# Moving the gate projection behind attention and the SSM tables into attention, in a hybrid attention and S5 encoder layer

## The chip, the core and the metric

The kernel runs on one core of a Trainium2 chip. The metric is the time of one execution in microseconds (us), lower is better. The engines have these names in the rows: PE is TensorE (PEld its weight loads), DVE is VectorE, ACT is ScalarE, POOL is GpSimd, SP is SyncE, which here only issues DMAs. A name with a q behind it (SPq, PEq) is the sequencer of that engine.

## The reference, cut to what matters

One encoder layer over 2048 tokens of width 1024, all in float32. The parts that the change touches are these:

```python
h = rmsnorm(x, norm_mix_pre)
z = h @ w_in                            # 1024 x 3328: [q | k | v | u | gates]
q, k, v, u, gates = jnp.split(z, splits, axis=-1)   # 512, 128, 128, 512, 2048 columns
y_attn = windowed_gqa_sink(q, k, v, attn_sink) @ w_branch_attn     # |t - s| <= 128, 8 heads, 2 kv heads
y_ssm = s5_bidirectional(u, ...) @ w_branch_ssm     # scan in both directions, + D*u, GELU, GLU
g = jax.nn.sigmoid(gates.reshape(bsz, seq, 2, 1024))
merged = g[:, :, 0] * y_attn + g[:, :, 1] * y_ssm
# then w_out, a norm, and a gated feed-forward part of width 2816 with a 3-tap convolution
```

The S5 part has 32 groups of 16 channels with 64 complex states each. The kernel computes it in chunks of 8 tokens: tables of powers of the transition take a chunk's inputs into its state (`into`), a scan runs over the 256 chunk states, further tables take the state before a chunk to its outputs (`outof`), and `local` covers what tokens of one chunk do to each other.

## The kernel before, in words

Every large matrix product is made from split operands: `split_products` (L322) multiplies w_hi by x_hi, w_lo by x_hi and w_hi by x_lo, so three matmuls of 128x512 for each 128 rows of the contraction. A block of 128 output rows by 2048 tokens has 4 chunks of 512 tokens and 8 contraction steps, so 96 matmuls. `WeightStream` (L282) loads a block's weights (SyncE), rounds them to w_hi (L315) and subtracts to w_lo (L317) on VectorE, in two slots.

The stages run one after the other with a barrier between them (L64):

- `stage_project_in`: norm and transposition of x into `feat_hi` and `feat_lo`, which stay in SBUF for the stage, and then 26 blocks: 6 for q, k, v, 4 for u, 16 for the gates. Beside them GpSimd computes the bases of the SSM tables (`bases.compute`) from small parameters that SyncE loads, and VectorE takes one reciprocal in it (`bases.invert`). In the SyncE queue these small loads stand ahead of the weights of block 2, and in the VectorE queue the reciprocal stands ahead of splitting them.
- `ssm_tables` (tiles `st_`): VectorE and GpSimd compute `b_table` and `outof` with complex products (L1170 to L1175), TensorE transposes, ScalarE copies, TensorE makes the `kernels`, and 16 DMAs spread them into `local`.
- `chunks_into_states` (tiles `si_`): 128 matmuls take u into the states, copied by ScalarE and VectorE.
- `attention_and_scan` (tiles `at_`): 16 blocks of 128 queries and 8 heads. For a head TensorE computes scores (L1770), VectorE masks them (L1861), ScalarE takes exponentials (L1967), TensorE transposes them (L1780), ScalarE copies (L1976), and TensorE multiplies by v (L1794). GpSimd runs the backward scan by itself. VectorE runs the forward scan in pieces between the masks. A scan has 45 steps of four parts (`ChunkScan.part`, L2067 to L2072): 15 large steps inside blocks of 16 chunks, 15 small ones over the blocks, 15 large ones into the next block.
- `states_to_outputs` (tiles `so_`): 16 pairs of groups, matmuls with `local` and `outof`, GELU on ScalarE, 64 stores by SyncE.
- then `stage_branches` (tiles `br_`), `stage_out`, `stage_gate_up` and `stage_down`, which stay as they are.

The order on each engine is that of the code; nothing is scheduled by a program.

Of the kernel before, what the change touches and what calls it, by code (L numbers as in the profile page):

```python
# [21 lines left out]
F32 = mybir.dt.float32  # L22
F32R = mybir.dt.float32r
# [22 lines left out]
WARM_UP = 72  # L46
# [283 lines left out]
def stage_project_in(nc, x, gain, w_in, qkv, u_scratch, gate_scratch, bases):  # L330
# [3 lines left out]
    with ExitStack() as ctx:  # L334
# [10 lines left out]
        n_qkv, n_u, n_gate = qkv.shape[0] // P, SSM // P, 2 * D // P  # L345

        parts = [(0, n_qkv, qkv, "plain"), (n_qkv, n_u, u_scratch, "by chunk"),
                 (n_qkv + n_u, n_gate, gate_scratch, "sigmoid")]
        n_blocks = n_qkv + n_u + n_gate
# [9 lines left out]
        @block.sync  # L359
        def _(sync):  # L360
            nt.load(sync, ws, [(s, w_in, slice(s * P, (s + 1) * P)) for s in range(2)])

            sync.wait_ge(nt.turned, TILES + 2)
            bases.load(nc, sync)
            with sync.Fori(1, n_blocks // 2) as i:
                for s in range(2):
                    ws.load(sync, w_in, s, i * 2 + s, bass.ds((i * 2 + s) * P, P))

        @block.vector
        def _(dve):  # L370
            nt.vector(dve, turn_psum, ws)
            bases.invert(dve)
            with dve.Fori(1, n_blocks // 2) as i:
                for s in range(2):
                    ws.vector(dve, s, i, i * 2 + s)
# [23 lines left out]
        def _(act):  # L399
# [4 lines left out]
            for first, count, dest, kind in parts:  # L404
                dest_rows = dest.rearrange("(b p) t -> b p t", p=P)
                with act.Fori(0, count // 2) as i:
                    for s in range(2):
# [4 lines left out]
                        for c in range(CHUNKS):  # L412
# [9 lines left out]
                            func = ACT.Sigmoid if kind == "sigmoid" else ACT.Copy  # L422
                            act.activation(out, src, func).then_inc(chunk_free, 1)  # L423
# [964 lines left out]
def stage_mixers(nc, qkv, sink, attn_scratch, u_scratch, bases, ssm_d, y_scratch):  # L1388
# [3 lines left out]
    with ExitStack() as ctx:  # L1392
        m = Pool(nc, ctx, "sm")

        outof = [[m.sb(f"outof{d}{r}", [P, QS, POWERS, SSM_CH]) for r in range(2)] for d in range(2)]

        region = m.sb("region", [P, 2 * 2 * QS * P])
        u_region = m.sb("u_region", [P, GROUPS * SSM_J])
        u = u_region[:].rearrange("p (g j) -> p g j", g=GROUPS)
        into = region[:].rearrange("p (d q e r n) -> p d q e r n", d=2, q=QS, e=2, r=2)  # L1400
        local = m.sb("local", [P, GROUPS, LC])
        with ExitStack() as part:
            ssm_tables(nc, Pool(nc, part, "st"), bases, ssm_d, u_scratch, u, outof, into, local)

        states = [m.sb(f"states{d}", [P, 2, QS, SSM_J + 1]) for d in range(2)]
        scans = [ChunkScan(m, d, states[d], bases.leaps[d], d == 1) for d in range(2)]
        with ExitStack() as part:
            chunks_into_states(nc, Pool(nc, part, "si"), u, into, states)
        with ExitStack() as part:
            lost = attention_and_scan(nc, Pool(nc, part, "at"), region, u_region, qkv, sink, attn_scratch, scans)  # L1410
        with ExitStack() as part:
            states_to_outputs(nc, Pool(nc, part, "so"), region, u, lost, u_scratch, y_scratch, outof, local, states)


def ssm_tables(nc, m, bases, ssm_d, u_scratch, u, outof, into, local):
# [842 lines left out]
```

## Time and profile before

| | before |
|---|---|
| median of 3 runs | 3148.57 us (3147.24 to 3149.11) |
| the profiled execution, its own time | 3148.73 us |
| its span in the trace | 3147.2 us |
| mean granted TensorE clock, share of full speed | 0.957 |
| busy share of the span: PE, PEld | 90%, 73% |
| busy share: DVE, ACT, POOL | 37%, 23%, 16% |

The span reaches from the first to the last instruction; the profiled execution took 1.5 us more than that. A busy share is a mean over stages with different limits, and PE counts as busy while a matmul is in its pipeline, so the shares alone don't tell what a stage waits for. The stages have to be read one by one.

### The profile page before, as it was taken

To read this page: it belongs to the slowest core of one execution; us is meant where nothing else is said; L and a number is where in the kernel's file an instruction comes from. 1 tells how busy PE (TensorE), PEld (TensorE's weight loads), DVE (VectorE), ACT (ScalarE), POOL (GpSimd) and SP (SyncE) were. 2 spreads that over 40 slices of the span, in tenths; PEclk is the share of its full clock that TensorE was granted. 3 is DMA by queue.
4 is the path that set the end of the run, shared out by engine and by line. 5 is a ranking of instruction groups with operands and counts; after the bars stand their busy time and mean duration, and the time that the engine had idled before them with its cause. 6 is when DMAs were issued, how large, how long until landed. Compare 5 with 4: busy or idle time off the path is not lost. (4 is left out here: it accounts for less than half of the span.)

```text
span 3147.2 us, 36636 instructions
## 1 busy us (share of the span) xinstructions
PE 2831.1 (90%) x13014; PEld 2310.1 (73%) x13014; DVE 1161.7 (37%) x1392; ACT 709.8 (23%) x1144; POOL 509.1 (16%) x829
## 2 busy tenths in 40 slices
PE   6699999945898778989948999999999997999998
PEld 5588888835666557867847888888888885888886
DVE  5000000065999816434334322223223233224342
ACT  4012111122454324002123111111111112213221
POOL 2440000062788600001111000000000001000111
PEclk9899999977999989999969999999999998999999
DMA  4312212142111172435442111111111115434653
GB/s 127 81 60 80 78 62 80 52 89 27 48 59 47 34 186 104 170 136 181 145 122 81 53 33 53 53 47 53 34 52 53 47 40 165 116 96 126 178 165 122
DMA packets 298549, 278.18 MB, mean 88 GB/s; under 512 B 46592, under 2 KB 270080, under 8 KB 288768
## 3 DMA queue, kind: packets, MB, share of 16 engines
q1 hardware_dynamic: 253792, 160.94, 18.4%
q0 software_dynamic: 13248, 68.16, 6.1%
q10 hardware_dynamic: 31456, 48.42, 5.0%
q8 instruction: 28, 0.46, 0.1%
q14 instruction: 25, 0.20, 0.0%
HBM read 191.50 MB, written 83.89 MB: 88 GB/s over the span
## 5 line engine op out<-in xcount | busy, mean ns | idle before, releaser
L325 PE MATMUL gu_banks<-gu_feat_hi,gu_w_hi 128*128 128x512 f32 (+1 forms) x1408 | 549.4, 390 | 1.0 <-DVE gu_feat_lo L235 1.0
L327 PE MATMUL gu_banks<-gu_feat_lo,gu_w_hi 128*128 128x512 f32 (+1 forms) x1408 | 548.4, 389 | 0.0
L326 PE MATMUL gu_banks<-gu_feat_hi,gu_w_lo 128*128 128x512 f32 (+1 forms) x1408 | 548.3, 389 | 0.0
L325 PE MATMUL pi_banks<-pi_feat_hi,pi_w_hi 128*128 128x512 f32 (+1 forms) x832 | 326.8, 393 | 31.0 <-DVE pi_w_lo L317 30.0
L327 PE MATMUL pi_banks<-pi_feat_lo,pi_w_hi 128*128 128x512 f32 (+1 forms) x832 | 325.0, 391 | 0.0
L326 PE MATMUL pi_banks<-pi_feat_hi,pi_w_lo 128*128 128x512 f32 (+1 forms) x832 | 325.0, 391 | 0.0
L325 PEld LDWEIGHTS gu_banks<-gu_feat_hi,gu_w_hi 128*128 128x128 f32 x1408 | 264.6, 188 | 55.9 <-DVE gu_feat_lo L235 1.4
L327 PEld LDWEIGHTS gu_banks<-gu_feat_lo,gu_w_hi 128*128 128x128 f32 x1408 | 264.5, 188 | 55.2
L326 PEld LDWEIGHTS gu_banks<-gu_feat_hi,gu_w_lo 128*128 128x128 f32 x1408 | 264.6, 188 | 54.4
L325 PE MATMUL dn_y<-dn_w_hi,dn_f_hi 128*128 128x512 f32 x704 | 276.3, 393 | 23.4 <-DVE dn_w_lo L801 23.3
L326 PE MATMUL dn_y<-dn_w_hi,dn_f_lo 128*128 128x512 f32 x704 | 275.4, 391 | 0.0
L327 PE MATMUL dn_y<-dn_w_lo,dn_f_hi 128*128 128x512 f32 x704 | 275.3, 391 | 0.0
L315 DVE CAST gu_w_hi<-gu_w_raw 128x1024 fp32r<-128x1024 f32 x44 | 30.5, 693 | 619.2 <-PE gu_banks L327 619.2
L325 PEld LDWEIGHTS pi_banks<-pi_feat_hi,pi_w_hi 128*128 128x128 f32 x832 | 157.3, 189 | 64.0 <-issue 30.4
L504 ACT ACTIVATE gu_gate<-gu_banks 128x512 f32<-128x512 f32 x88 | 52.7, 601 | 596.2 <-PE gu_banks L327 596.2
L315 DVE CAST pi_w_hi<-pi_w_raw 128x1024 fp32r<-128x1024 f32 x26 | 18.1, 695 | 446.5 <-PE pi_banks L327 437.9
L423 ACT ACTIVATE pi_rows_out<-pi_banks 128x512 f32<-128x512 f32 x104 | 70.0, 676 | 496.3 <-PE pi_banks L327 496.3
L327 PEld LDWEIGHTS pi_banks<-pi_feat_lo,pi_w_hi 128*128 128x128 f32 x832 | 156.9, 189 | 32.9
L326 PEld LDWEIGHTS pi_banks<-pi_feat_hi,pi_w_lo 128*128 128x128 f32 x832 | 157.2, 189 | 32.4
L325 PEld LDWEIGHTS dn_y<-dn_w_hi,dn_f_hi 128*128 128x128 f32 x704 | 133.2, 189 | 53.2 <-issue 19.2
L557 POOL DMA_DIRECT2D f<-gu_conv x22 | 11.8, 535 | 936.5 <-DVE gu_conv L539 936.5
L327 PEld LDWEIGHTS dn_y<-dn_w_lo,dn_f_hi 128*128 128x128 f32 x704 | 133.1, 189 | 28.1
(237 smaller groups left out, 4237.7 us busy)
## 6 DMA issues: line engine op xcount, KB each, us to landing
dn_f_raw<-f SPq DMA_DIRECT2D x64, 704.0 KB, 5.9
f<-gu_conv POOLq DMA_DIRECT2D x22, 1024.0 KB, 4.1
gates<-pi_rows_out ACTq DMA_DIRECT2D x16, 1024.0 KB, 4.3
br_rows<-gates POOLq DMA_DIRECT2D x16, 1024.0 KB, 7.0
pi_w_raw<-in_w_in SPq DMA_DIRECT2D x26, 512.0 KB, 4.8
gu_w_raw<-in_w_ffn_gate SPq DMA_DIRECT2D x22, 512.0 KB, 3.8
gu_w_raw<-in_w_ffn_up SPq DMA_DIRECT2D x22, 512.0 KB, 3.8
dn_w_raw<-in_w_ffn_down POOLq DMA_DIRECT2D x22, 512.0 KB, 6.9
```

What stands on the lines that cost most here:

```text
L315: dve.tensor_copy(self.hi[:, s], self.raw[:, s]).then_inc(self.hi_ready, 1)
L325: pe.matmul(out, w_hi, x_hi, start=first, stop=False)
L326: pe.matmul(out, w_lo, x_hi, start=False, stop=False)
L327: return pe.matmul(out, w_hi, x_lo, start=False, stop=last)
L423: act.activation(out, src, func).then_inc(chunk_free, 1)
L504: act.activation(gate[:, 1 + c * BANK:1 + (c + 1) * BANK], banks[:, c, :], ACT.Copy)\
L557: pool.dma_start(f_rows[i], conv[:]).then_inc(stored, 16)
```

## The change

Three things are done together.

1. `stage_project_in` makes only the 10 blocks of q, k, v and u. The weights of blocks 2 and 3 are loaded and split ahead of the small loads and the reciprocal of the bases. Between later weight loads SyncE stores `feat_hi` and `feat_lo` to DRAM, 8 DMAs of 2 MB.
2. `attention_and_tables` replaces `ssm_tables` and the attention stage. The head loop is written out; a slot is one head of one block (128 slots). VectorE makes a piece of the table products in two of three slots (8 of the 16 columns, in groups of 4), GpSimd the other 8 columns in a row, TensorE puts the transpositions and kernel products into numbered slots, all through one PSUM bank `t_psum`. The warm-up of TensorE (72 transpositions) is gone. `outof` and `local` are stored to DRAM at the stage's end, all by SyncE.
3. `gates_and_states` (tiles `gs_`) makes the states, then the 16 gate blocks as 64 parts of 24 matmuls, token chunk by token chunk, so that the gate weights are loaded four times over (64 loads of 512 KB for 16). ScalarE rounds the weights and takes the sigmoid, VectorE subtracts. GpSimd and VectorE scan meanwhile, VectorE three parts for each gate part. Features come back from DRAM chunk by chunk; then `outof`, `local` and u, and the outputs follow without a barrier.

```diff
-        n_qkv, n_u, n_gate = qkv.shape[0] // P, SSM // P, 2 * D // P
+        n_qkv, n_u = qkv.shape[0] // P, SSM // P
...
+            for b in range(2, 4):
+                ws.load(sync, w_in, b % 2, b, slice(b * P, (b + 1) * P))
             sync.wait_ge(nt.turned, TILES + 2)
             bases.load(nc, sync)
-            with sync.Fori(1, n_blocks // 2) as i:
-                for s in range(2):
-                    ws.load(sync, w_in, s, i * 2 + s, bass.ds((i * 2 + s) * P, P))
+            for b in range(4, n_blocks):
+                ws.load(sync, w_in, b % 2, b, slice(b * P, (b + 1) * P))
+                if b % 2:
+                    continue
+                c = (b - 4) // 2
+                store_features(c)
...
+    DVE_COLUMNS = [slice(0, QS // 4), slice(QS // 4, QS // 2)]
+    POOL_COLUMNS = [slice(QS // 2, QS)]
+    C_AT = {10 + n: n for n in range(4)}
+    INTO_AT = {**{20 + 2 * n: n for n in range(8)}, **{38 + 2 * n: 8 + n for n in range(8)}}
+    KERNELS_AT = {**{56 + 2 * n: n for n in range(K_BANKS)}, **{78 + 2 * n: K_BANKS + n for n in range(K_BANKS)}}
...
+                if slot - 1 in KERNELS_AT:
+                    keep_kernels(KERNELS_AT[slot - 1])
+                elif slot == DIAG_AT:
+                    add_diagonal()
+                if slot % 3 != 2:
+                    next(own_tables, None)
...
+        for n in range(N_PARTS):
+            c, s = n // N_BLOCKS, n % 2
+            if n % N_BLOCKS == 0:
+                pe.wait_ge(feat_in[c % 2], (c // 2 + 1) * 2 * KD * 16)
+            pe.wait_ge(w_lo_ready, n + 1)
+            if n >= 2:
+                pe.wait_ge(gate_free, n - 1)
+            for k in range(KD):
+                done = split_products(pe, banks[:, 6 + s, :], w_hi[:, s, k], w_lo[:, s, k],
+                                      feat[c % 2][:, 0, k], feat[c % 2][:, 1, k], k == 0, k == KD - 1)
+            done.then_inc(gate_done, 1)
...
+        def split_hi(n):
+            act.wait_ge(w_raw_in[n % 2], n // 2 * 16 + 16)
+            if n >= 2:
+                act.wait_ge(gate_done, n - 1)
+            act.activation(w_hi[:, n % 2], w_raw[:, n % 2], ACT.Copy).then_inc(w_hi_ready, 1)
...
+        for n in range(N_PARTS):
+            if n + 2 < N_PARTS:
+                split_lo(n + 2)
+            for _ in range(3):
+                next(own_scan, None)
```

Three places of the instruction order show it. First SyncE in the input projection: ahead, the weights of block 2 and later (`pi_w_raw`) stand behind the loads of the bases' parameters (`pi_normed`).

```order
L1276 DMA pi_normed<-in_b_im_f 128x16x16
L1276 DMA pi_normed<-in_b_re_b 128x16x16
L1276 DMA pi_normed<-in_b_im_b 128x16x16
L365 UNCONDITIONAL_BRANCH
L365 ISA
L301 ISA
L301 DMA pi_w_raw<-in_w_in 128x8x128
```

In the changed kernel two weight loads stand ahead of them, and the feature stores follow between the later ones:

```order
L300 DMA pi_w_raw<-in_w_in 128x8x128 x2
L1280 DMA pi_normed<-in_lam_re_f 128x16x1
L1282 DMA pi_normed<-in_lam_im_f 128x16x1
L1286 DMA pi_normed<-in_log_dt_f 64x16x1 x2
L1280 DMA pi_normed<-in_lam_re_b 128x16x1
L1282 DMA pi_normed<-in_lam_im_b 128x16x1
L1286 DMA pi_normed<-in_log_dt_b 64x16x1 x2
L1290 DMA pi_normed<-in_b_re_f 128x16x16
L1290 DMA pi_normed<-in_b_im_f 128x16x16
L1290 DMA pi_normed<-in_b_re_b 128x16x16
L1290 DMA pi_normed<-in_b_im_b 128x16x16
L300 DMA pi_w_raw<-in_w_in 128x8x128
```

The loads for blocks 2 and 3 have moved from behind the parameters to ahead of them. Second VectorE in attention, before: a mask (two ISA rows, L1861) and then one part of the scan, for each head.

```order
L1861 ISA sm_region,at_neg_top<-at_s_psum,sm_region,at_neg_sinks 128x385
L1861 ISA at_neg_top 128x1
L2067 TENSOR_TENSOR sm_by_im<-sm_states,bases 128x512
L1861 ISA sm_region,at_neg_top<-at_s_psum,sm_region,at_neg_sinks 128x385
L1861 ISA at_neg_top 128x1
L2069 TENSOR_TENSOR sm_states<-sm_states,sm_by_re 128x32x16
```

In the changed kernel a piece of the tables stands where the scan part stood, and in each third slot nothing:

```order
L1867 ISA at_neg_scores,at_neg_top<-at_s_psum,at_bias,at_neg_sinks 128x385
L1867 ISA at_neg_top 128x1
L1434 TENSOR_TENSOR at_table_temp<-bases 128x4x128
L1867 ISA at_neg_scores,at_neg_top<-at_s_psum,at_bias,at_neg_sinks 128x385
L1867 ISA at_neg_top 128x1
L1867 ISA at_neg_scores,at_neg_top<-at_s_psum,at_bias,at_neg_sinks 128x385
L1867 ISA at_neg_top 128x1
L1437 TENSOR_TENSOR at_outof<-at_outof,at_table_temp 128x512
```

The third place is VectorE in the new stage: the scan parts (L2352 to L2357) stand three by three between the subtractions that make w_lo (L2272), each for one gate part.

```order
L2272 TENSOR_TENSOR gs_w_lo<-gs_w_raw,gs_w_hi 128x1024
L2352 TENSOR_TENSOR bases<-gs_states,bases 128x512 x2
L2354 TENSOR_TENSOR gs_states<-gs_states,bases 128x32x16
L2272 TENSOR_TENSOR gs_w_lo<-gs_w_raw,gs_w_hi 128x1024
L2356 TENSOR_TENSOR gs_states<-gs_states,bases 128x16x16
L2357 TENSOR_TENSOR gs_states<-gs_states,bases 128x16x16
```

The scan has moved from between the masks to between the weight splits of the gates.

## Rows read from the trace of the kernel before

**Rows 1.** Windows by stage: us, busy time (instructions), TensorE clock, DMA, GB/s.

```profile
0.00:123.95 123.95, 67.36 (x320) 54.17 (x321) 44.98 (x39) 38.94 (x57) 25.48 (x91) 0.88 0.41 111
123.95:267.90 143.95, 143.95 (x626) 118.95 (x627) 13.63 (x14) 19.53 (x26) 64.36 (x199) 0.98 0.23 73
267.90:648.60 380.70, 380.70 (x1680) 314.91 (x1678) 30.72 (x32) 55.62 (x78) 0.00 (x0) 1.00 0.20 66
648.60:654.30 5.70, 0.00 (x0) 0.00 (x0) 0.00 (x0) 0.60 (x1) 0.00 (x0) 0.68 0.45 184
654.30:758.80 104.50, 33.45 (x208) 30.57 (x208) 71.57 (x37) 15.05 (x32) 70.67 (x29) 0.66 0.49 71
758.80:791.80 33.00, 30.08 (x128) 25.81 (x128) 27.18 (x66) 24.26 (x64) 0.01 (x1) 0.93 0.00 1
791.80:804.20 12.40, 9.75 (x72) 9.52 (x73) 10.09 (x15) 1.28 (x1) 8.57 (x11) 0.86 0.33 96
804.20:1095.70 291.50, 253.20 (x1470) 182.06 (x1470) 275.56 (x553) 143.34 (x400) 231.63 (x220) 0.98 0.15 45
1095.70:1099.70 4.00, 0.00 (x0) 0.00 (x0) 0.00 (x0) 0.59 (x1) 0.00 (x0) 0.77 0.22 66
1099.70:1149.50 49.80, 49.09 (x320) 36.36 (x320) 0.00 (x0) 10.84 (x17) 0.00 (x0) 0.95 0.73 117
```

**Rows 2.** Timeline of TensorE where block 2 begins: start us, us, idle before.

```profile
123.95 0.79 PE L325 MATMUL pi_banks<-pi_feat_hi,pi_w_hi 128*128 128x512 f32 x1 [30.00 <-DVE pi_w_lo L317]
```

**Rows 3.** Timeline of VectorE, two weight splits one block apart.

```profile
148.16 0.69 DVE L315 CAST pi_w_hi<-pi_w_raw 128x1024 fp32r<-128x1024 f32 x1 [22.14 <-PE pi_banks L327]
...
169.92 0.69 DVE L315 CAST pi_w_hi<-pi_w_raw 128x1024 fp32r<-128x1024 f32 x1 [19.80 <-PE pi_banks L327]
```

**Rows 4.** Timeline of SyncE's DMA issues: last weights of the projection, `local`.

```profile
116.82 447.33 SPq L301 DMA_DIRECT2D pi_w_raw<-in_w_in  x24
...
738.34 9.54 SPq L1464 DMA_DIRECT2D sm_local<-st_kernels  x8
```

**Rows 5.** DMA issues: count, KB each, median us from issue to landing.

```profile
f<-gu_conv POOLq DMA_DIRECT2D x22, 1024.0 KB, 4.1
...
pi_w_raw<-in_w_in SPq DMA_DIRECT2D x26, 512.0 KB, 4.8
```

**Rows 6.** Timeline of the weight loads, scores of two heads, one after the other.

```profile
944.86 0.30 PEld L1770 LDWEIGHTS at_s_psum<-sm_region 128*128 128x128 f32 x2
...
946.51 0.30 PEld L1770 LDWEIGHTS at_s_psum<-sm_region 128*128 128x128 f32 x2
```

**Rows 7.** Timeline of VectorE, the reciprocal that each query block has once.

```profile
936.98 0.19 DVE L1894 RECIPROCAL at_share<-at_sums 128x8 f32<-128x8 f32 x1
...
951.80 0.19 DVE L1894 RECIPROCAL at_share<-at_sums 128x8 f32<-128x8 f32 x1
```

**Rows 8.** VectorE by line and shape, attention: busy us, mean ns, idle before.

```profile
L1861 DVE CUSTOM_DVE_ANT_0 sm_region<-at_s_psum,sm_region,at_neg_sinks 128x385 f32<-128x385 f32 x112 | 67.9, 606 | 0.2 <-issue 0.2
...
L2069 DVE TENSOR_TENSOR sm_states<-sm_states,sm_by_re 128x512 f32 x12 | 20.3, 1692 | 0.0
...
L2067 DVE TENSOR_TENSOR sm_by_re<-sm_states,bases 128x512 f32<-128x512 f32 x15 | 19.9, 1325 | 0.0
...
L2072 DVE TENSOR_TENSOR sm_states<-sm_states,sm_by_im 128x256 f32 x12 | 13.3, 1112 | 0.0
...
L2071 DVE TENSOR_TENSOR sm_states<-sm_states,sm_by_im 128x256 f32 x12 | 8.0, 669 | 0.0
```

**Rows 9.** VectorE by line, the table products: busy us, mean ns.

```profile
L1173 DVE TENSOR_TENSOR sm_outof<-bases,st_c_t 128x1440 f32<-128x1440 f32 x2 | 6.7, 3346 | 0.1
...
L1170 DVE TENSOR_TENSOR st_b_table<-bases 128x1408 f32<-128x1408 f32 x2 | 4.2, 2075 | 47.4 <-PEq L64 47.3
```

**Rows 10.** VectorE by line, the weight subtraction of the projection.

```profile
L317 DVE TENSOR_TENSOR pi_w_lo<-pi_w_raw,pi_w_hi 128x1024 fp32r<-128x1024 f32 x26 | 32.0, 1231 | 0.9
```

**Rows 11.** Timeline of TensorE, the first half of the kernel products.

```profile
726.92 9.93 PE L1618 MATMUL st_banks<-sm_outof,st_b_pair 128*32 128x128 f32 x64 [9.85 <-POOLq L1543]
```

More of the change, by code:

```diff
@@ L45 @@
 CHUNKS = TOK // BANK
-WARM_UP = 72
 SSM_L = 8
@@ L1402, in stage_mixers @@
         with ExitStack() as part:
-            ssm_tables(nc, Pool(nc, part, "st"), bases, ssm_d, u_scratch, u, outof, into, local)
-        states = [m.sb(f"states{d}", [P, 2, QS, SSM_J + 1]) for d in range(2)]
-        scans = [ChunkScan(m, d, states[d], bases.leaps[d], d == 1) for d in range(2)]
+            attention_and_tables(nc, Pool(nc, part, "at"), qkv, sink, attn_scratch, bases, ssm_d, u_scratch,
+                                 whole_u(u_region), into_region, into, outof_scratch, local_scratch)
@@ L1407, in stage_mixers @@
         with ExitStack() as part:
[L1408 to L1415, printed above, removed]
-    ident = m.sb("ident", [P, P])
+            gates_and_states(nc, Pool(nc, part, "gs"), u_region, into_region, into, u_scratch, feat_scratch, w_gates,
+                             gate_scratch, outof_scratch, local_scratch, bases, y_scratch)
@@ L1625, in attention_and_scan @@
[L1625 to L1650 removed]
+    bias = m.sb("bias", [P, N_HEADS, WIDE])
@@ new lines, in make_kernels @@
+        def make_kernels(n):
+            d, part = n // K_BANKS, n % K_BANKS
+            k0 = 0 if d == 0 else 1
+            if part == 0:
+                pe.wait_ge(outof_ready[d], 2)
+            if n:
+                pe.wait_ge(kernels_copied, n)
+            else:
+                pe.wait_ge(into_copied, 16)
+                pe.wait_ge(b_pair_ready, 8)
+            for j in range(PER_BANK):
+                w = part * PER_BANK + j
+                for r in range(2):
+                    done = pe.matmul(t_psum[0:2 * SSM_CH, j * LC:(j + 1) * LC],
+                                     b_pair[:, d, r, w].rearrange("p e c -> p (e c)"),
+                                     outof[d][r][:, w, k0:k0 + SSM_L].rearrange("p k c -> p (k c)"),
+                                     start=r == 0, stop=r == 1)
+            done.then_inc(kernels_done, 1)
@@ L2072, in part, with steps @@
             engine.tensor_tensor(target[:, 1:2], target[:, 1:2], by_im[:, 0:1], ALU.add).then_inc(done, 1)
+    def steps(self):
+        for i in range(SCAN_I - 1):
+            yield self.within(i)
+        for i in range(SCAN_J - 1):
+            yield self.of_last(i)
+        for i in range(SCAN_I - 1):
+            yield self.into_next(i)
     def over_blocks(self, engine):
@@ L2227, in hybrid_layer @@
     f = scratch("f", (FF, TOK))
+    feats = [scratch(f"feat_{part}", (CHUNKS, P, KD, BANK)) for part in ("hi", "lo")]
+    outof = [scratch(f"outof{n}", (P, QS * POWERS * SSM_CH)) for n in range(4)]
+    local = scratch("local", (P, GROUPS, LC))
     params = [[t[f"{name}_{direction}"] for name in LAM_NAMES] for direction in "fb"]
```

1022 lines of the change are left out of this document (565 added, 457 removed).

## The prediction

> **What bounds the kernel now.** I read the windows by stage first [rows 1]. In the input projection TensorE is busy throughout from 123.95 us at the full clock of 2.4 GHz, while DVE is at a tenth and GpSimd ends within the second window: there TensorE alone sets the time. In the table stage (654.3 to 758.8) it is the other way round: DVE and GpSimd are busy for 72 and 71 of 104.5 us, TensorE for 33 at a clock of 0.66, and the last 20 us are one group of DMAs [rows 1, 4]. In attention DVE is busy for 275.6 of 291.5 us and GpSimd for 231.6, and what fills DVE is the scan between the masks. So two kinds of stage stand one after the other, one bound by TensorE and two bound by DVE, and the reader is to see that the change lays them beside each other. Second, TensorE sits idle for 30 us before block 2 of the projection [rows 2], since its weights are issued only at 116.82 us, behind the parameter loads [rows 4].
>
> **The projection.** Block 2 started at 123.95 after 30.00 us of idle time, so block 1 ended at 93.95. With the weights of blocks 2 and 3 ahead of the parameters nothing stands between. A block takes 169.92 - 148.16 = 21.76 us [rows 3]. Eight blocks remain: 93.95 + 8 x 21.76 = 268.0, where 648.6 stood. The bases on GpSimd are done within the window that ends at 267.9 [rows 1], so they stay covered by little; were they 10 us later, the stage would be too. The weights of block 4 are issued where those of block 2 were (116.82) and are due at 137. Behind them the 4 MB of one chunk's features go out: 1 MB landed in 4.1 us [rows 5], so at most 17 us, and block 5 is due at 159. The stores are hidden by the blocks; uncovered, the 16 MB would cost 66 us. The barrier keeps its 5.7 us: next stage at 273.7.
>
> **Attention with tables.** The prologue stays 12.4 us, since it ends with DVE's preparation, not with the warm-up of 9.75 us that is removed [rows 1]: first score at 286.1. The warm-up gone, TensorE starts cold; in the table stage its clock averaged 0.66 and in the next 0.93, so I allow 1 us (bounds 0 and 5).
>
> TensorE's pace is 946.51 - 944.86 = 1.65 us a head where its weight loads follow each other [rows 6]; with the transpositions of v and of the output a block needs about 14.0. In the lightest scan phase, where every head still has five small operations on DVE, a block took 951.80 - 936.98 = 14.8 [rows 7]. I take 14.5 for each of 14 middle blocks, 203 us, and an estimate of 10 for each of the two outer blocks, which have two thirds of the keys. DVE can follow: for a head the mask is 0.61 [rows 8], and a table piece of 512 or 576 elements is, scaled from [rows 9], 2075 x 512/1408 = 0.75 to 3346 x 576/1440 = 1.34 us, two of them in three slots: 1.1 to 1.5 us for a head, plus 0.2 for the rest of the block, against 1.75 on TensorE.
>
> TensorE's added work comes on top, since TensorE now sets the pace: 80 transpositions at 9.75/72 = 0.135 us [rows 1] are 11, and the kernel products are 128 instructions at 9.93/64 = 0.155 [rows 11], 20, or some 17 at a full clock. With 3 us for the last head's chain: 203 + 20 + 11 + 17 + 3 + 1 = 255, to 541.1, where 291.5 stood. Bounds: 245 if the blocks run at 14.0, 290 if the mask chain sets the pace as before.
>
> **The end of that stage.** The stores of `outof` (4.7 MB) and of `local` (16 DMAs) stand in SyncE's queue behind the loads of the last block, which wait for block 13. That is some 29 us before TensorE's end. Before, `local` took 20.5 us from 738.34 to 758.8, issued by two engines in 9.54 us for eight each [rows 1, 4]; now SyncE issues all sixteen, 19 us. Loads 4, `outof` up to 19 (4.7 x 4.1), `local` 20 gives 43, so 14 us behind the compute; part of `outof` may go faster, and I take 11 (bounds 4, as the attention store alone had [rows 1], and 20). Next stage at 552.1.
>
> **States and gates.** The 128 matmuls into the states keep their 30.1 us [rows 1]: TensorE is at 582.2. Two weight splits ride along. Then 64 parts of 24 matmuls: 21.76/4 = 5.44 us each, 348 us, the same TensorE work that left the projection. Beside each part DVE has one subtraction, 1.23 us [rows 10], and three quarters of a scan step. A large step is 2 x 1.325 + 1.692 + 0.669 + 1.112 = 6.12 us [rows 8], so 4.6 for three parts; together 5.8, and 5.9 with the waits of operations that now follow their own results directly (estimate). This is over 5.44, in 40 of 64 parts (the two large phases, 60 of 180 scan parts each); in the other 24 DVE has room. Cost: 40 x 0.46 = 18 us, so 366 us, to 948.2. What covers the scan is TensorE; DVE has 30 x 6.12 + 15 small steps of some 1.5 = 206 us of scan and 79 of subtractions in hand here, 285, which is what it would cost uncovered. GpSimd's scan, 231.6 us busy in 291.5, ends some 70 us before the gates do. Bounds for the stage: 348, and 366 plus 40 parts at 1.2 us more.
>
> One rule of the Trainium skill speaks against this place. In the rows DVE was busy for 275.6 and GpSimd for 231.6 of 291.5 us [rows 1], so they overlapped for at least 215.6 us and did not shut each other out. The Trainium skill (GPSIMD Engine Reference, section 8, Key points) says that GpSimd shares its SBUF interfaces with VectorE, with contention for DVE instructions that have two SBUF inputs. The masks had one input in PSUM; in the new stage every DVE operation but the copies has two inputs in SBUF. Taken strictly it would add the two engines' times; the trace disagrees with that, and whether more contention comes than before no run here shows yet.
>
> Weights: a slot comes free when DVE has subtracted, and is wanted again about 7 us later (two parts, 10.9, less 4 for rounding, subtraction and a wait); the 512 KB landed in 4.8 us [rows 5]. Traffic is 512 KB of weights, up to 512 KB of features and 256 KB of output in 5.44 us, 235 GB/s, while 1 MB in 4.1 us is 250 GB/s for a single DMA [rows 5]. I cost it at nothing, with 5 us over the whole as the upper bound of the likeliest case; late weights would stall TensorE directly.
>
> **Outputs.** 49.8 us before, with TensorE cold at the start and 0.95 in the mean [rows 1]. Now it comes warm from the gates: 47, plus 1.5 for the reload of u, which is issued only after the last gate: 996.7, where 1149.5 stood. All stages behind it are unchanged.
>
> **Sum.** 996.7 - 1149.5 = -152.8 us. The profiled execution took 3148.73 (the span of 3147.2 and 1.5 around it), which is the median of the runs (3148.57) within 0.2: 2996. By stages: projection -380.6, table stage -104.5, attention -36.5, its end +7, states -2.9 (DVE's tail and the barrier), gates +366, outputs -1.3.
>
> **Rivals.** Likeliest (0.62): as above, 2975 to 3020.
>
> DVE slows more beside GpSimd (0.15). For it: all its operations there have two SBUF inputs. Against: GpSimd was as busy before. If a part takes 6.9 instead of 5.9: 40 more, 3036. At the far end the two engines exclude each other: 231.6 of GpSimd, 206 of scan and 64 x 1.23 of subtractions are 517 instead of 366, 3147, which is no change.
>
> Weights or features late (0.08). For it: weights are loaded four times over, and the feature loads stand in the same queue. At 6.6 us a part, 64 x 0.9 = 58 more: 3054.
>
> Attention keeps its pace (0.08): the chain mask, exponential, transposition, copy sets 285 instead of 255, and the result is 3026.
>
> Slower than before (0.05): the same late weights, further. The break-even is 152.8/64 = 2.4 us over 366/64 = 5.7, so 8.1 us for each part. Two slots turn over in 16.2 us; less a ScalarE rounding, DVE's 1.23 and a wait for a scan part of up to 1.7, a weight load would have to take 12 us from issue to landing, at 4.8 now. At 9 us a part the kernel takes 3205. The rest (0.02) is within noise of no change.
>
> **How the numbers follow.** The predicted time is that of the likeliest case. The range takes in the fast bounds (attention 245, no DVE excess in the gates, store tail 4: 2961) and the two middle rivals up to about 3050: 2962 to 3050. A difference of 0.2% (6 us) is about what can be told from none. Faster 0.94, same 0.01, slower 0.05: all cases but the last two are faster by over 1%.
>
> **What would show it.** Right: the projection ends near 268 with no idle time before block 2; first score near 286; query blocks 14.5 us apart; table DMAs ending some 10 us behind the last matmul of attention; gate parts at 5.4 us in the middle third and 5.9 at both sides, with TensorE waiting for w_lo and DVE never idle there. Wrong: TensorE waiting for the weights' DMA behind ScalarE, scan operations well over 1.3 us, or the head pace over 2 us.

## The result and the profile after

The changed kernel takes 3066.13 us (median of 4 runs, 3063.82 to 3068.0), beside 3148.84 us for the kernel before (4 runs, 3147.24 to 3149.43). The ratio is 0.9738, with a 95% interval of 0.9726 to 0.9749. So it is faster, by 83 us where 153 were forecast, and 3066 lies 16 us outside the range of 2962 to 3050. The time of every run below is a median, with the lowest and the highest execution behind it; a single execution of the kernel with four edits, 7377.14 us where its five others took 2981 to 2984, is left out of its median.

The windows by stage, cut where the stages of the changed kernel begin and end, answer to [rows 1] and have its columns: us, busy time of PE, PEld, DVE, ACT and POOL with their instructions, TensorE clock, DMA share, GB/s.

```profile
94.00:124.00 30.00, 30.00 (x134) 24.86 (x133) 1.58 (x2) 2.99 (x5) 3.10 (x11) 1.00 0.37 81
124.00:267.50 143.50, 143.26 (x633) 118.28 (x631) 11.54 (x12) 23.26 (x27) 70.76 (x217) 1.00 0.51 185
267.50:273.40 5.90, 0.00 (x0) 0.00 (x0) 0.00 (x0) 0.83 (x1) 0.00 (x0) 0.79 0.43 178
273.40:295.70 22.30, 0.66 (x2) 0.29 (x2) 20.17 (x15) 0.00 (x0) 18.88 (x14) 0.50 0.44 102
295.70:552.00 256.30, 248.88 (x1676) 202.03 (x1676) 148.26 (x389) 158.57 (x432) 44.54 (x19) 0.99 0.35 90
552.00:566.50 14.50, 0.02 (x1) 0.05 (x1) 0.00 (x0) 0.49 (x1) 0.00 (x0) 0.58 0.67 103
566.50:599.10 32.60, 31.36 (x127) 24.26 (x128) 27.44 (x63) 25.31 (x64) 0.00 (x0) 0.93 0.61 194
599.10:1009.20 410.10, 365.35 (x1539) 294.68 (x1539) 323.42 (x293) 98.86 (x129) 268.38 (x238) 0.96 0.53 168
1009.20:1068.80 59.60, 49.61 (x321) 35.94 (x319) 0.00 (x0) 10.87 (x18) 0.00 (x0) 0.91 0.71 115
```

Read them against the forecast, stage by stage:

| stage | forecast, us | measured, us | difference |
|---|---|---|---|
| projection and barrier, from 0 | 273.7 | 273.4 | -0.3 |
| prologue of attention | 12.4 | 22.3 | +9.9 |
| attention with tables | 255 | 256.3 | +1.3 |
| its end | 11 | 14.5 | +3.5 |
| into the states | 30.1 | 32.6 | +2.5 |
| 64 gate parts | 366 | 410.1 | +44.1 |
| outputs | 48.5 | 59.6 | +11.1 |
| end of the outputs | 996.7 | 1068.8 | +72.1 |

The stages behind the outputs, which the change leaves alone, took 1.5 us less than before (1996.2 for 1997.7). The projection and attention came out as forecast. In the gates TensorE is busy for 365 of 410 us, and VectorE for 323 where 285 were forecast for its whole work.

The ScalarE operations that take a gate part's sigmoid show each part's end. Their distance is 5.44 us, within 0.3 but for two shorter ones (4.0 and 4.4) at the two ends, except in three places: 15 parts from 622.37 to 743.56 us take 121.2 instead of 81.6 (+39.6), 5 parts from 879.55 to 916.17 take 36.6 instead of 27.2 (+9.4), and 3 parts from 916.17 to 945.12 take 29.0 instead of 16.3 (+12.6). In the first place both engines make the large steps of their first phase (GpSimd from 602 to 739 us, VectorE from 608 to 754), in the second those of their last one (GpSimd until 909.98, VectorE from 865), and it ends six us after GpSimd's scan does.

The timeline of VectorE and GpSimd in the middle of the first place, for a weight subtraction and two parts of the scan:

```profile
654.38 1.83 DVE L2272 TENSOR_TENSOR gs_w_lo<-gs_w_raw,gs_w_hi 128x1024 fp32r<-128x1024 f32 x1
655.46 1.93 POOL L2352 TENSOR_TENSOR bases<-gs_states,bases 128x512 f32<-128x512 f32 x1 [0.33 <-POOL gs_states L2357]
656.13 2.17 DVE L2354 TENSOR_TENSOR gs_states<-gs_states,bases 128x512 f32<-128x512 f32 x1
657.57 1.79 POOL L2352 TENSOR_TENSOR bases<-gs_states,bases 128x512 f32<-128x512 f32 x1 [0.18 <-POOL bases L2352]
658.33 1.49 DVE L2356 TENSOR_TENSOR gs_states<-gs_states,bases 128x256 f32<-128x256 f32 x1
```

Add start and duration: GpSimd's operations end at 657.39 and 659.36, VectorE's at 658.30 and 659.82. Each VectorE operation begins while one of GpSimd runs and ends 0.91 or 0.46 us behind its end. That is a little less than these operations take by themselves (1.05 and 0.61, measured below), as if they had waited for that end: the two engines go in step, one operation against one. It holds throughout this phase. Of VectorE's operations on 512 elements between 620 and 740 us, 34 began while one of GpSimd's ran; they lasted 1.07 to 2.40 us, but all of them ended 0.81 to 1.00 us behind GpSimd's end. The same engines where GpSimd's scan ends (909.98 us):

```profile
907.50 1.79 DVE L2272 TENSOR_TENSOR gs_w_lo<-gs_w_raw,gs_w_hi 128x1024 fp32r<-128x1024 f32 x1
908.17 1.81 POOL L2357 TENSOR_TENSOR gs_states<-gs_states,bases 128x240 f32 x1
909.22 1.62 DVE L2354 TENSOR_TENSOR gs_states<-gs_states,bases 128x480 f32<-128x480 f32 x1
910.88 0.58 DVE L2356 TENSOR_TENSOR gs_states<-gs_states,bases 128x240 f32<-128x240 f32 x1
911.99 1.01 DVE L2352 TENSOR_TENSOR bases<-gs_states,bases 128x480 f32<-128x480 f32 x1
912.91 1.21 DVE L2272 TENSOR_TENSOR gs_w_lo<-gs_w_raw,gs_w_hi 128x1024 fp32r<-128x1024 f32 x1
```

From the first line to the last the subtraction falls from 1.79 to 1.21 us. In the prologue it is plainer still: 8 one-input operations on 384 elements, 6.48 us together before, now stand beside a memset and the table products of GpSimd. The first line is all 8 together.

```profile
278.10 15.39 DVE L1923 TENSOR_SCALAR at_bias<-at_distance_f 128x384 f32<-128x384 f32 x8 [1.34 <-POOL at_distance_f L1702]
...
281.96 2.02 POOL L1434 TENSOR_TENSOR at_table_temp<-bases 128x1024 f32<-128x1024 f32 x1
284.06 2.34 POOL L1437 TENSOR_TENSOR sm_into_region<-sm_into_region,at_table_temp 128x1024 f32<-128x1024 f32 x1
```

The mean of 1.92 us hides three kinds. The first operation took 1.92 beside GpSimd's memset of 1.81, six took 2.16 to 2.50 beside table products of 2.02 to 2.34, each ending 0.20 us behind its product, and the last, which began between two products, took 0.35. These 8 give 8.9 of the +9.9 of the prologue, and one more operation behind them (1.98 us for 0.81, L1926 now and L1933 before) gives the rest.

The third place of the gates is another matter. What holds the gates there is ScalarE waiting for the weights' DMA (its wait in total, times and longest, from 600 to 1010 us, and the landing times of that tile):

```profile
ACT gs_w_hi L2238 <- DMA gs_w_raw<-in_w_in: 17.8, 1, 17.8
...
DMA to landing us min/median/max: 3.6/4.5/20.4
```

Windows of 5 us around it, whose last two numbers are the busy share of the DMA engines and GB/s:

```profile
905.00:910.00 5.00, 3.06 (x14) 2.24 (x13) 4.97 (x4) 1.54 (x2) 4.77 (x4) 1.00 0.19 59
910.00:915.00 5.00, 5.00 (x24) 4.12 (x23) 4.93 (x6) 0.00 (x0) 2.85 (x5) 1.00 1.04 241
915.00:920.00 5.00, 5.00 (x24) 4.14 (x23) 4.90 (x7) 1.55 (x2) 0.00 (x0) 1.00 1.05 436
...
925.00:930.00 5.00, 0.98 (x5) 0.48 (x3) 0.00 (x0) 0.00 (x0) 0.00 (x0) 0.97 1.02 420
```

At 910 us GpSimd, done with its scan, issues five loads at once (four of `outof`, one of `local`, 6.7 MB), and the DMA engines are full until 930 (shares of 0.99 to 1.05). The weight load issued at 914.15 lands 20.4 us later, where the median is 4.5; the next one, issued at 918.41, takes 17.5.

### The profile page after: what moved, and what is told of

Its sections match the earlier page's. It is cut to its first block and busy times, and to the rows that moved or that the text cites. A ratio compares the mean times of both kernels' runs of the same rounds, so it can differ in the third digit from the quotient of the medians.

```text
span 3065.0 us, 35647 instructions
## 1 busy us (share of the span) xinstructions
PE 2799.5 (91%) x12942; PEld 2293.0 (75%) x12942; DVE 1266.1 (41%) x1448; ACT 760.4 (25%) x1200; POOL 530.8 (17%) x840
## 5 line engine op out<-in xcount | busy, mean ns | idle before, releaser
L325 PEld LDWEIGHTS dn_y<-dn_w_hi,dn_f_lo 128*128 128x128 f32 x704 | 133.1, 189 | 27.6
L2352 POOL TENSOR_TENSOR bases<-gs_states,bases 128x512 f32<-128x512 f32 (+2 forms) x90 | 109.6, 1218 | 202.9 <-POOLq L2373 179.6
L2238 ACT ACTIVATE gs_w_hi<-gs_w_raw 128x1024 fp32r<-128x1024 f32 x64 | 67.9, 1060 | 302.6 <-PE gs_banks L326 284.3
L763 ACT ACTIVATE dn_f_hi<-dn_f_raw 128x1408 fp32r<-128x1408 f32 x64 | 85.2, 1372 | 204.0 <-PE dn_y L326 163.0
L2272 DVE TENSOR_TENSOR gs_w_lo<-gs_w_raw,gs_w_hi 128x1024 fp32r<-128x1024 f32 x64 | 104.3, 1629 | 74.1 <-ACT gs_w_hi L2238 74.0
L324 PE MATMUL gs_banks<-gs_feat,gs_w_hi 128*128 128x512 f32 x256 | 104.8, 410 | 26.0 <-DVE gs_w_lo L2272 26.0
L324 PE MATMUL pi_banks<-pi_feat_hi,pi_w_hi 128*128 128x512 f32 (+1 forms) x320 | 126.2, 394 | 1.0 <-DVE pi_feat_lo L234 1.0
L326 PE MATMUL pi_banks<-pi_feat_lo,pi_w_hi 128*128 128x512 f32 (+1 forms) x320 | 125.1, 391 | 0.0
```

Source lines behind the costliest of these rows:

```text
L324: pe.matmul(out, w_hi, x_hi, start=first, stop=False)
L325: pe.matmul(out, w_lo, x_hi, start=False, stop=False)
L326: return pe.matmul(out, w_hi, x_lo, start=False, stop=last)
L763: act.activation(f_hi[:, s, h * KH:(h + 1) * KH], f_raw[:, h], ACT.Copy)\
L2238: act.activation(w_hi[:, n % 2], w_raw[:, n % 2], ACT.Copy).then_inc(w_hi_ready, 1)
L2272: dve.tensor_tensor(w_lo[:, n % 2], w_raw[:, n % 2], w_hi[:, n % 2].bitcast(F32), ALU.subtract)\
```

## The experiments

SBUF is the on-chip memory in which the kernel keeps its tables, weights and states, PSUM the one into which its matmuls write. Theory A is the hold: a VectorE operation whose inputs all lie in SBUF waits for the GpSimd operation beside it to end, and one with an input in PSUM does not. The rivals are that VectorE by itself is too slow for three scan parts and a subtraction (theory B, my forecast), that the handover from ScalarE sets the pace (C), and that the engines share bandwidth by the element. A gain is counted from the 3066.13 us of the changed kernel; a ratio is to the kernel before, measured in the same round, with its 95% interval.

**GpSimd's scan left out of the gates** (the backward states are then only the chunk inputs).

```diff
-        scans[1].run(pool)
+        pool.sem_inc(scans[1].done, STEPS)
```

> GpSimd's backward scan is left out of the gates stage (the kernel's backward states are then only the chunk inputs); all else stays. In the changed kernel the gate parts stand 5.44 us apart except in three stretches: 15 parts take 121.2 us while GpSimd makes its first large phase (+39.6 over 5.44 each), 5 take 36.6 while it makes its last large phase (+9.4), and three take 29.0 around the wait for a weight load (+12.6). Theory A, an operation of VectorE on SBUF is held until the GpSimd operation beside it ends: all gate parts at 5.44, the 512-element scan products at 1.05 to 1.1 us instead of 1.75, w_lo at 1.21; the weight-load wait stays or goes. 3066 - 49 = 3017 us, or 3004 if the wait goes too. Theory B, VectorE is by itself too slow for three scan parts and a subtraction (my forecast of 5.9 us a part): 40 parts at 5.9, about 3035. Theory C, the parts are slow for the handover from ScalarE and not for GpSimd: 3066.

3004.35 us (3002.47 to 3006.29, ratio 0.9541, 0.9526 to 0.9555), 61.8 less. From the fifth gate part on the parts stand at 5.44 us (two of them 0.3 off and one 4.4), but for the wait for weights. That wait is +2.2 now and was +12.6: with no scan ahead of them, two of the five loads go out at the stage's start, and only three come at once. So about 49 us of the gain are the hold and 10.4 the wait; the last 2 are not placed. VectorE by line and shape in the gates, busy us and mean ns, first of the changed kernel:

```profile
L2272 DVE TENSOR_TENSOR gs_w_lo<-gs_w_raw,gs_w_hi 128x1024 fp32r<-128x1024 f32 x62 | 101.8, 1642 | 74.1 <-ACT gs_w_hi L2238 74.0
L2352 DVE TENSOR_TENSOR bases<-gs_states,bases 128x512 f32<-128x512 f32 x30 | 52.3, 1745 | 0.7
...
L2354 DVE TENSOR_TENSOR gs_states<-gs_states,bases 128x512 f32<-128x512 f32 x15 | 26.9, 1793 | 0.3
```

and without GpSimd's scan:

```profile
L2272 DVE TENSOR_TENSOR gs_w_lo<-gs_w_raw,gs_w_hi 128x1024 fp32r<-128x1024 f32 x62 | 76.0, 1225 | 125.8 <-ACT gs_w_hi L2238 125.8
L2352 DVE TENSOR_TENSOR bases<-gs_states,bases 128x512 f32<-128x512 f32 x30 | 31.2, 1039 | 0.7
L2354 DVE TENSOR_TENSOR gs_states<-gs_states,bases 128x512 f32<-128x512 f32 x15 | 15.8, 1052 | 0.3
```

B and C fall: by itself VectorE has room beside every gate part, and ScalarE's work is the same here. This run takes away all of GpSimd's scan, though, so it does not say in what way GpSimd slows VectorE.

**VectorE's scan in PSUM.** During the gates three PSUM banks of the states are idle. They take the two product buffers and the table of factors, so every scan operation has an input in PSUM; GpSimd's scan runs as before.

```diff
-    scans = [ChunkScan(m, d, states[d], bases.leaps[d], d == 1, by[f"by{2 * d}"], by[f"by{2 * d + 1}"])
-             for d in range(2)]
...
+    in_psum = [banks[:, n].rearrange("p (r q j) -> p r q j", r=2, q=QS) for n in range(2)]
+    leaps = banks[:, 2].rearrange("p (n k q) -> p n k q", n=2, q=QS)
+    scans = [ChunkScan(m, 0, states[0], leaps, False, in_psum[0], in_psum[1]),
+             ChunkScan(m, 1, states[1], bases.leaps[1], True, by["by2"], by["by3"])]
...
-        dve.sem_inc(scans[0].done, 1)
+        dve.wait_ge(into_copied[1], 2 * GROUPS)
+        dve.tensor_copy(leaps, bases.leaps[0]).then_inc(scans[0].done, 1)
```

> VectorE's scan keeps its table of factors and both product buffers in three idle PSUM banks, so each of its scan operations has an operand in PSUM; GpSimd's scan stays as it is. Theory A (VectorE operations on SBUF alone are held until GpSimd's operation ends, those with a PSUM input are not, as the masks show): only the subtraction w_lo is still held, the 512-element products take 1.1 to 1.3 us, gate parts 5.44 to 5.7 in the first large phase; 3020 us, 3012 to 3030. Theory B (the two engines share the bandwidth, wherever the operand lies, or VectorE is too slow by itself): no gain, 3060 to 3070, or a few us slower if PSUM operands are slower.

3014.63 us (3012.14 to 3015.64, ratio 0.9573, 0.9558 to 0.9588), 51.5 less. Every gate part stands at 5.44 us again but for the wait for weights (+11.9), though GpSimd scans as before. The step between the two engines is gone too: of VectorE's scan operations on 512 elements from 620 to 740 us, all take 1.03 to 1.13 us, and their ends lie anywhere from 0.48 us ahead of GpSimd's end to 0.92 behind it.

**Only the products in PSUM**, the factors in SBUF.

```diff
+    in_psum = [banks[:, n].rearrange("p (r q j) -> p r q j", r=2, q=QS) for n in range(2)]
+    scans = [ChunkScan(m, 0, states[0], bases.leaps[0], False, in_psum[0], in_psum[1]),
...
```

> Only the two product buffers of VectorE's scan lie in PSUM; the factors stay in SBUF. So two of five operations of a step read two SBUF operands and write PSUM, three read one SBUF and one PSUM operand. If what holds an operation is that its inputs are all in SBUF, the products stay at about 1.8 us and the additions fall to 1.1, 0.6 and 0.6: 6.0 for a large step instead of 7.5, parts of 6.5 in the first large phase, about 3036 us. If one operand in PSUM is enough wherever it is, the output too, it is as fast as with the factors in PSUM, about 3020. If PSUM changes nothing, 3066.

3037.69 us (3036.66 to 3039.12, ratio 0.9647, 0.9632 to 0.9661), 28.4 less. In the first large phase 15 gate parts take 6.3 to 6.9 us, as the first of the three forecasts had it. VectorE by line and shape, first with all in PSUM:

```profile
L2274 DVE TENSOR_TENSOR gs_w_lo<-gs_w_raw,gs_w_hi 128x1024 fp32r<-128x1024 f32 x61 | 91.0, 1491 | 112.1 <-ACT gs_w_hi L2240 112.1
L2355 DVE TENSOR_TENSOR gs_banks<-gs_states,gs_banks 128x512 f32<-128x512 f32 x30 | 32.0, 1066 | 0.7
```

and with the products alone there:

```profile
L2354 DVE TENSOR_TENSOR gs_banks<-gs_states,bases 128x512 f32<-128x512 f32 x30 | 55.6, 1855 | 0.7
L2356 DVE TENSOR_TENSOR gs_states<-gs_states,gs_banks 128x512 f32<-128x512 f32 x15 | 16.3, 1086 | 0.3
```

With GpSimd scanning beside it, a product of 512 elements takes 1.07 us if one input is in PSUM and 1.86 if both are in SBUF and only the output is in PSUM. The input decides. With all in PSUM the subtraction, both of whose inputs stayed in SBUF, is still held (1.49 in the mean, 1.23 alone), but the gate parts have room for that.

**GpSimd's table products halved in attention.**

```diff
-    POOL_COLUMNS = [slice(QS // 2, QS)]
+    POOL_COLUMNS = [slice(QS // 2, 3 * QS // 4), slice(3 * QS // 4, QS)]
```

> GpSimd makes its table products in attention in pieces of 4 columns instead of 8: twice as many operations, half as long (an estimate of 1.05 us for 2.02). Theory A (a VectorE operation on SBUF ends when the GpSimd operation beside it ends): the 8 bias operations of the prologue take about 1.2 us each instead of 2.2, the first score stands 7 us earlier, and the table pieces of VectorE shorten too: 3058 us, 3052 to 3062. Theory B (the engines share bandwidth, element by element): GpSimd moves as many elements in as long a time, the 8 operations keep 15.4 us, 3066.

3057.84 us (3055.68 to 3059.94, ratio 0.9711, 0.9698 to 0.9725), 8.3 less. Timeline of VectorE and GpSimd:

```profile
278.85 9.58 DVE L1923 TENSOR_SCALAR at_bias<-at_distance_f 128x384 f32<-128x384 f32 x8 [1.33 <-POOL at_distance_f L1702]
...
281.80 1.10 POOL L1434 TENSOR_TENSOR at_table_temp<-bases 128x512 f32<-128x512 f32 x1
```

The same elements in shorter operations, and VectorE's 8 operations go from 15.39 to 9.58 us. The six beside table products take 1.24 to 1.42 us instead of 2.16 to 2.50, and each ends 0.21 us behind the product beside it; the one beside the memset, which was not cut, keeps its 1.93. What is held is one operation for one operation, not bandwidth.

**GpSimd's tables after the bias.**

```diff
+        pool.wait_ge(bias_step, 5 + N_HEADS)
         pool.memset(b_pair[:], 0.0).then_inc(b_pair_zero, 1)
```

> GpSimd starts its fill of b_pair and its table products in attention only when VectorE has made the bias tables. Theory A (VectorE's bias operations were held by GpSimd's): the 8 operations take 0.35 us each, 2.8 instead of 15.4, the first score comes 10 to 12 us earlier, at about 285, and GpSimd's later start is hidden, since it is idle for 21 us before its second table: 3056 us, 3052 to 3059. Theory B (the preparation waits for something else, the loads of q and k): the first score moves by less than 3 us, 3063 to 3066.

3054.02 us (3050.83 to 3057.7, ratio 0.9698, 0.9685 to 0.9712), 12.1 less.

```profile
278.94 2.24 DVE L1924 TENSOR_SCALAR at_bias<-at_distance_f 128x384 f32<-128x384 f32 x8 [1.34 <-POOL at_distance_f L1702]
```

0.28 us from one to the next. The gain of 12.1 is more than the loss of 9.9, so the prologue of the kernel before, where the same 8 took 6.48 us, was held too.

**The tables' reload spread.** `outof`'s last part and `local` load before the scan, the others one by one.

```diff
-        scans[1].run(pool)
-
         pool.wait_ge(into_done, GROUPS)
...
-        pool.wait_ge(gate_done, LATE_AT)
+        scans[1].run(pool)
+
         for n in range(3):
+            pool.wait_ge(gate_done, LATE_AT + 5 + 3 * n)
             pool.dma_start(outof_flat[n], outof_scratch[n]).then_inc(tables_in, 16)
```

> The reload of the tables: outof's last part and local are loaded before GpSimd's scan, and the other three parts of outof one by one, at gate parts 53, 56 and 59, instead of all 5 in one go at 910 us. Theory D (five table DMAs issued at once, 5.7 MB, held up one 512 KB weight load for 18 us): the stretch of three parts that took 29.0 us takes 16.3 to 19, so 3054 us, 3051 to 3058. Theory E (that weight load was late because its slot came free late): no change, 3066.

(The five loads are 6.7 MB; the expectation left 1 MB out.) 3054.57 us (3050.83 to 3057.03, ratio 0.97, 0.9687 to 0.9713), 11.6 less. The weights' landing is 9.1 us at most, and from 917.65 us on every gate part stands at 5.45 or less. Theory D holds and E falls.

**u back in three parts.** SyncE and ScalarE each issue half of the first two; SyncE alone issues the third, ahead of the stores of y.

```diff
-    u_parts = [slice(middle, first_u), slice(0, middle)]
+    u_parts = [slice(first_u - 4, first_u), slice(middle, first_u - 4), slice(0, middle)]
```

> After the last gate u comes back in three parts, the first of 4 groups instead of 12 (8 DMAs of 64 KB each), so TensorE waits for 0.5 MB and not for 1.6. If the wait of 9.9 us is the volume in front of the groups that are wanted first: 3 us or less remain, and the matmuls run warm; 3058 us, 3054 to 3061. If it is the time of issuing and landing whatever the size: 3064 to 3066.

3067.93 us (3063.47 to 3069.73, ratio 0.9738, 0.9725 to 0.9752): no change from 3066.13, where the expectation had 3058. TensorE's waits in the outputs were one line, and became two:

```profile
PE gs_banks L2197 <- DMA sm_u_region<-u: 9.9, 1, 9.9
```

```profile
PE gs_banks L2199 <- ACT bases L2265: 3.9, 1, 3.9
PE gs_banks L2199 <- DMA sm_u_region<-u: 3.3, 2, 1.7
```

The wait for u fell to 3.3, but behind the loads stand the stores of y, ScalarE waits for one of them for a free buffer (10.3 us), and TensorE for ScalarE.

**`outof` and half of `local` stored by GpSimd** (in the diff `store_local` is the loop over the 8 DMAs of one half; the four stores of `outof` move likewise).

```diff
-        for e in range(2):
-            for l in range(SSM_L):
+        store_local(sync, 0, local_placed)
...
+        store_local(pool, 1, pool_placed)
```

> The stores of outof and half of those of local move from SyncE to GpSimd, which is idle from 422 us. SyncE issued 16 of local in 32 us, 2.0 each, from 529.6 to 561.6, while the last head was done at 552. If the issuing queue sets the tail: local ends at about 548, the next stage starts some 5 us behind the attention store, at 557 instead of 566.4: 3057 us, 3055 to 3060. If the DMAs themselves need the time (small rows): 3064 to 3067.

3056.37 us (3055.09 to 3058.75, ratio 0.9707, 0.9693 to 0.972), 9.8 less. SyncE's DMA issues, in the changed kernel and here:

```profile
526.29 3.24 SPq L1635 DMA_DIRECT2D outof<-at_outof  x4
529.57 32.05 SPq L1641 DMA_DIRECT2D local<-at_kernels  x16
566.44 1.02 SPq L2112 DMA_DIRECT2D gs_w_raw<-in_w_in  x2
```

```profile
526.04 9.14 SPq L1599 DMA_DIRECT2D local<-at_kernels  x8
555.70 1.02 SPq L2116 DMA_DIRECT2D gs_w_raw<-in_w_in  x2
```

An issue of `local` took 2.0 us right behind the four large stores, and 1.14 here. GpSimd does not only have another queue, it also issues earlier: `outof` from 422 to 445 us and its half of `local` at 487, where SyncE came to them at 526 and 530. So the queue, the earlier start, the smaller number of issues and the large stores still under way at 530 are not told apart, and which of the two parts of the edit did more was not tried either.

**Four edits together** (scan in PSUM, tables after the bias, reload spread, stores on GpSimd).

> Four edits of the changed kernel at once: VectorE's scan with factors and products in PSUM, GpSimd's tables after the bias, the reload of outof spread, the stores of outof and half of local on GpSimd. Alone they gave 51.5, 12.1, 11.6 and 9.8 us. They lie in four different places, so they should add up: 3066.1 - 85 = 2981 us, 2975 to 2987. If the places that they free only uncover one another (a later wait takes over), 2990 or more.

2981.65 us (five executions, 2980.97 to 2983.64, ratio 0.9472, 0.946 to 0.9484). The four gains add up (85.0 expected, 84.5 found).

**The same, and u's third part by GpSimd, late.**

> The four edits and the reload of u in three parts again, but the third part (12 groups) is issued by GpSimd only after three pairs of outputs, so that it stands neither ahead of the stores of y in SyncE's queue nor in front of the groups wanted next. With the third part in front, the wait for u fell from 9.9 to 1.7 and 1.7 us, but 3.9 came for ScalarE, which waited for stores of y, and the time did not change. If that queueing ate the gain: 6 to 8 us less than with four edits alone, 2974. If the volume of DMA traffic in the output part is the limit: the same as with four edits, within 2 us.

2978.61 us (2977.32 to 2979.98, ratio 0.9462, 0.9449 to 0.9474): 3.0 us less, half or less of the 6 to 8 that queueing alone was to give. TensorE's wait for u falls from 9.5 to 1.2 us, but it still waits 4.7 us for ScalarE, once, and ScalarE 9.4 us for a store of y, though the third part of u no longer stands ahead of it. So the queue was part of it. The DMA engines seem to be the rest: with the four edits alone the profile has them at a busy share of 1.14 with only 191 GB/s while u comes back. That was not tested.

**The kernel before, without GpSimd's scan.**

```diff
-        scans[1].run(pool)
+        pool.sem_inc(scans[1].done, 1)
```

> The kernel before, with GpSimd's backward scan left out of attention. If the durations of VectorE's scan in the kernel before held the wait for GpSimd in them, so that the rows of before that I priced the scan from were not VectorE's own pace: the 512-element products fall from 1.325 to 1.04 us, the large addition from 1.69 to 1.05, the last of the four parts from 1.11 and 0.67 to 0.61 and 0.60, the 8 bias operations of the prologue from 6.48 to about 2.3 us, and attention takes about 45 us less, 3105. If VectorE ran at its own pace there: the durations stay within 5% and the time at 3147.

3094.42 us in one execution, some 54 less than the kernel before and 11 less than expected. VectorE by line and shape in attention, to be read against [rows 8]:

```profile
L2067 DVE TENSOR_TENSOR sm_by_re<-sm_states,bases 128x512 f32<-128x512 f32 x15 | 15.6, 1037 | 0.0
...
L2069 DVE TENSOR_TENSOR sm_states<-sm_states,sm_by_re 128x512 f32 x12 | 12.6, 1050 | 0.0
...
L2071 DVE TENSOR_TENSOR sm_states<-sm_states,sm_by_im 128x256 f32 x12 | 7.3, 608 | 0.0
```

The durations fall from 1.325 to 1.04 and from 1.69 to 1.05, the 8 operations of the prologue from 6.48 to 2.24, and the query blocks of the first large phase stand 14.1 us apart instead of 17.1. The masks, with one input in PSUM, stay as they were (0.613 us in the mean, 0.606 in [rows 8]). VectorE's rows of before were held rows.

## Why the prediction was wrong

**The projection was right.** TensorE has no idle time where block 2 begins (busy for 30.00 us of 94 to 124), and the next stage begins at 273.4, where 273.7 was forecast. The feature stores and the bases are hidden.

**The failed step: the price of the scan beside GpSimd.** "A large step is ... 6.12 us [rows 8]. So 4.6 for three parts; together 5.8, and 5.9 with the waits". Two things were wrong in it. First, the price was not VectorE's own: alone a large step is 2 x 1.04 + 1.05 + 0.61 + 0.60 = 4.34 us, and 6.12 had the hold in it. Second, I carried it over as if it were a property of the operation. In attention nearly each scan part stood behind a mask, whose input in PSUM is not held, so that 0.6 us of a hold could pass under the mask (the lines of before below show one). In the gates scan parts and subtractions follow one another, all of them held: in the first large phase 2 x 1.745 + 1.793 + 1.301 + 0.921 = 7.5 us for a large step, and 1.64 for a subtraction in the mean of the stage. The term was 18 us and measured 49, and not spread over 40 parts but in 20 of those in which both engines make large steps; where either makes small steps, or GpSimd none, a part takes 5.44. With the 12.6 us of the weights below, these 31 us are the +44.1 of the gates. Taking GpSimd's scan away removes the loss, and moving one input of VectorE's scan to PSUM removes it with GpSimd still running (51.5 us).

My rival "DVE slows more beside GpSimd" had this mechanism at 0.15 and 3036 us; I argued against it that GpSimd was as busy before, which says nothing when the rows of before are slowed already. The sentence "so they overlapped for at least 215.6 us and did not shut each other out" was the root of it. A held operation is shown as busy, so two busy shares add up to overlap even where only one engine works at a time. The ends of single operations, side by side, showed it in the trace of before:

```profile
856.55 1.02 DVE L2067 TENSOR_TENSOR sm_by_im<-sm_states,bases 128x512 f32<-128x512 f32 x1
856.65 2.27 POOL L2069 TENSOR_TENSOR sm_states<-sm_states,sm_by_re 128x512 f32 x1 [0.33 <-POOL sm_by_im L2067]
857.49 0.60 DVE L1861 CUSTOM_DVE_ANT_0 sm_region<-at_s_psum,sm_region,at_neg_sinks 128x385 f32<-128x385 f32 x1
858.02 1.80 DVE L2069 TENSOR_TENSOR sm_states<-sm_states,sm_by_re 128x512 f32 x1
```

VectorE's product came first and took 1.02 us. GpSimd's addition began beside it and ended at 858.92, after 2.27 us. The mask kept its 0.60 in the meantime. VectorE's addition then began while GpSimd's still ran, and ended 0.90 us behind its end. In the whole of attention before, 37 operations of VectorE on 512 elements began while one of GpSimd's ran; they lasted 1.03 to 2.10 us, and every one ended 0.81 to 1.03 us behind GpSimd's end.

The rule for it was on another page of the Trainium skill than the one I weighed. The Trainium skill (SBUF — State Buffer, Who interferes with whom) says that VectorE and GpSimd lock the shared port for a whole instruction, whichever comes first, if the VectorE instruction has two SBUF inputs and GpSimd's reads SBUF, or if it is a copy, cast or `tensor_scalar` in a two-port mode, and that an instruction with at most one SBUF input outside these modes does not contend. The trace agrees in each case that ran: two SBUF inputs 1.86 us against 1.07 with one in PSUM, a one-input `tensor_scalar` 2.16 to 2.50 against 0.35, and GpSimd itself late where VectorE came first.

**The same hold in the prologue** (+9.9). "The prologue stays 12.4 us, since it ends with DVE's preparation". It does end there, but the preparation was priced as a constant, while the change put GpSimd's memset of 1.81 us and products of 2.0 to 2.3 beside it, where operations of 1.0 to 1.55 had stood. Since VectorE's short ones go one for one with GpSimd's, longer neighbours made it longer.

**Weights: "I cost it at nothing".** That held for every part but those beside the one burst, which cost 12.6 us. I had counted the weights, features and output of a gate part, and not the reload of `outof` and `local`, which stands in no steady state. Spreading it gave 11.6 us.

**The end of attention** (+3.5) was right in kind: SyncE issued `local` at 2.0 us each, not at 1.2 as priced [rows 4], and moving stores to GpSimd, which is idle and issues them earlier, gave 9.8 us. Why **into the states** took 2.5 us more than forecast no run tried.

**Outputs** (+11.1). "Plus 1.5 for the reload of u" had no row behind it. The loads land after 11.7 us (median on SyncE's queue), 3.1 MB for 24 groups, of which TensorE needs two first, so TensorE waited 9.9, and its granted clock was 0.59 in the mean from 1020 to 1030 us, in which the wait ended. That the wait was u is shown; how it could be had for nothing is not, since two ways to shorten it gave 0 and 3.0 us.

**Attention was right** at 256.3 for 255, and in part by luck. A block without extra work on TensorE takes 14.1 us there, where I took 14.5, and the 14 middle blocks with the added work took 226.7 us for 231; the outer blocks, with the first and the last head's chain, took 29.6 for 24. The holds are in it as well, but TensorE sets its pace and seems to cover them: halving GpSimd's operations changed the prologue and left the sum of the blocks as it was (236.3 us for 236.6, from the first block's reciprocal to the last's).

## What to carry to other kernels

A mean duration from a stage in which VectorE and GpSimd both work is a price of that pairing, not of the operation: compare the ends of single operations of both engines first, and if VectorE's always lie the same short time behind GpSimd's, price each VectorE operation at the rest of GpSimd's and its own time. Where GpSimd must run beside VectorE's critical work, give VectorE's operations an input in idle PSUM, or make GpSimd's operations short. And count the transfers that come once, at a phase's end, against the steady ones that they meet: here 6.7 MB issued at one moment cost 12 us where the weights' fourfold loading had cost nothing.

## What the runs showed of the hardware

- A VectorE `tensor_scalar` on 384 elements, 0.35 us alone, took 2.16 to 2.50 us beside GpSimd operations of 2.02 to 2.34 us, 1.24 to 1.42 beside operations of 1.10 to 1.26, and 1.92 beside a memset of 1.81. It begins at once in the trace and is shown as busy throughout.
- A VectorE operation on 512 elements with both inputs in SBUF, begun while GpSimd ran, ended 0.81 to 1.03 us behind GpSimd's end in both kernels, however long it was shown.
- An output in PSUM does not free it (1.86 us), an input does (1.07, where 1.04 is the time without GpSimd).
- GpSimd is held in its turn. With VectorE's scan in PSUM only the subtractions were left to hold it: of its products on 512 elements from 620 to 720 us, the six that began while a subtraction ran took 2.20 to 2.30 us and ended 1.19 to 1.23 us behind the subtraction's end, and all others took 1.32 to 1.39.
- 16 DMA issues of one shape took 2.0 us each right behind four large stores in the same queue. 8 of them took 1.14 each in the same queue where another had issued the large stores some 80 to 100 us before. Whether the queue or the stores under way cost the time is open.
